# A squared-ReLU perceptron by one level of Strassen's scheme (Winograd's form), and where its sums and the second layer's modulation are made

## What is computed

```python
mod = silu(c) @ w_mod[layer] + b_mod[layer]          # (1024) @ (1024, 6144)
h = rms_norm(x) * (1 + scale1) + shift1
x = x + gate1 * mixer(h)                             # layer 0: gated DeltaNet + attention, layer 1: RWKV-7
h = rms_norm(x) * (1 + scale2) + shift2
x = x + gate2 * (square(relu(h @ w_up[layer])) @ w_down[layer])   # (512,1024)@(1024,4096), (512,4096)@(4096,1024)
```

## Time and profile before

| | us |
|---|---|
| median of 3 runs (range) | 2294.35 (2292.71 to 2296.35) |
| the profiled execution | 2297.16 |
| its span, first to last instruction | 2295.5 |
| mean granted TensorE clock | 0.939 |
| PE busy | 2072.6 (90%) |
| DVE, ACT, POOL busy | 815.3, 395.5, 229.2 |

### The profile page before, as it was taken

How to read it: one execution, slowest core, us unless ns; L and a number is a source line. 1 busy time by engine, 2 the same in 40 slices (tenths; PEclk the granted TensorE clock), 3 DMA queues, 4 the chain that set the end, 5 groups by cost and what they waited for, 6 DMA issues and landing times.

```text
span 2295.5 us, 34406 instructions
## 1 busy us (share of the span) xinstructions
PE 2072.6 (90%) x14797; PEld 1078.1 (47%) x14797; DVE 815.3 (36%) x1449; ACT 395.5 (17%) x601; POOL 229.2 (10%) x145
## 2 busy tenths in 40 slices
PE   1988887876999999999779999999886999999998
PEld 1345455443444444444425666665673344444444
DVE  6656645237435220000163455555542111110000
ACT  1332213455020000000202222223311200000000
POOL 0000000000005787700000000000000000000000
PEclk7889998978999999999789999999996999999999
DMA  6421000010415554422101110110001222222222
GB/s 232 149 83 38 19 32 24 1 37 1 145 62 178 178 169 156 155 73 73 51 10 50 32 32 23 32 32 14 2 3 44 67 71 75 73 73 73 73 73 73
DMA packets 148063, 159.66 MB, mean 70 GB/s; under 512 B 8920, under 2 KB 136411, under 8 KB 147804
## 3 DMA queue, kind: packets, MB, share of 16 engines
q1 hardware_dynamic: 137052, 115.79, 16.2%
q0 software_dynamic: 10880, 41.95, 5.2%
HBM read 155.62 MB, written 2.10 MB: 69 GB/s over the span
## 4 chain that ended last, share of the span: by engine, by line
PE 80%; DVE 11%; ACT 5%; issue 2%; DMA 1%; SPq 0%; DVEq 0%; ACTq 0%
PE PS L449 80%; DVE arena L1356 2%; DVE arena L985 1%; DMA arena<-in_w_mod_dram 1%; DVE arena L1080 1%; ACT arena L1637 1%; ACT arena L1651 0%; DVE arena L1093 0%; ACT L1442 0%; DVE hT L1035 0%; DVE soft L1272 0%; SPq L351 0%; ACT hT L1457 0%; DMA arena<-in_w_in_dram 0%; DVE arena L1159 0%
## 5 line engine op out<-in xcount | busy, mean ns | idle before, releaser
L449 PE MATMUL PS<-arena 64*64 64x64 f32 (+4 forms) x11320 | 1190.9, 291 | 112.9 <-DVE arena L1093 23.4
L449 PEld LDWEIGHTS PS<-arena 64*64 64x64 f32 (+3 forms) x11320 | 665.9, 147 | 665.2 <-issue 537.7
L449 PE MATMUL PS<-hT,arena 128*128 128x512 f32 (+2 forms) x1504 | 683.7, 609 | 31.7 <-ACT hT L1457 12.1
L449 PEld LDWEIGHTS PS<-hT,arena 128*128 128x128 f32 (+2 forms) x1504 | 279.1, 190 | 372.5 <-issue 350.8
L1311 DVE SCALAR_TENSOR_TENSOR xT<-PS,gate_cols,xT 128x512 f32 x24 | 18.0, 751 | 493.6 <-PE PS L449 493.6
L1451 ACT ACTIVATE sq<-xT 128x512 f32<-128x512 f32 x32 | 20.2, 631 | 604.0 <-DVE xT L1311 305.9
L449 PE MATMUL PS<-sq,cst 128*128 128x512 f32 x152 | 84.4, 667 | 36.3 <-ACT sq L1451 30.7
L1746 POOL TENSOR_TENSOR arena<-arena,cond 128x2048 f32<-128x2048 f32 x24 | 86.6, 3609 | 28.4 <-DMA arena<-in_w_mod_dram 27.6
L1320 DVE TENSOR_SCALAR sq<-PS 128x512 f32<-128x512 f32 x32 | 22.1, 692 | 175.1 <-PE PS L449 175.1
L1712 ACT ACTIVATE arena<-PS 128x512 f32<-128x512 f32 x8 | 4.8, 598 | 451.6 <-PE PS L947 449.4
L1336 DVE TENSOR_SCALAR sq<-PS 128x512 f32<-128x512 f32 x32 | 22.1, 692 | 148.5 <-PE PS L449 148.4
(11 more groups left out here) (225 smaller groups left out, 1130.0 us busy)
## 6 DMA issues: line engine op xcount, KB each, us to landing
arena<-in_w_mod_dram POOLq DMA_DIRECT2D x40, 1024.0 KB, 5.8
arena<-in_w_up_dram SPq DMA_DIRECT2D x32, 1024.0 KB, 5.5
arena<-in_w_down_dram SPq DMA_DIRECT2D x32, 1024.0 KB, 5.3
arena<-in_w_mod_dram SPq DMA_DIRECT2D x8, 1024.0 KB, 5.0
arena<-in_w_in_dram SPq DMA_DIRECT2D x16, 512.0 KB, 3.7
arena<-in_w_out_dram SPq DMA_DIRECT2D x4, 1024.0 KB, 7.8
arena<-in_rwkv_w_r_dram SPq DMA_DIRECT2D x8, 512.0 KB, 4.0
arena<-in_rwkv_w_k_dram SPq DMA_DIRECT2D x8, 512.0 KB, 4.4
```

Source lines behind the costliest of these rows:

```text
L449: return pe.matmul(o, l, r, start=first, stop=last)
```

## The change

Each weight matrix is split in two by two quarters (input features, output features), the activations in two by two (input features, tokens 0 to 255 and 256 to 511), and Winograd's seven products take the place of eight. A perceptron is now 32 **units**: 16 for `up`, each making two tiles of 128 features by 512 tokens (`v` and `v + 16`), and 16 for `down`, four in a row (`c` = 0 to 3) adding up two output tiles (`p` and `p + 4`). One unit is seven products of four matmuls of 128 x 128 by **256** columns, each product in a bank of its own (banks 0 to 6). So a perceptron has 32 x 28 = 896 matmuls of 256 columns where it had 512 of 512.

- SyncE (`parts`): four DMAs per unit, 256 KB each with rows of 128 columns, into a ring of two units.
- VectorE: `weight_sums`, four additions of 128 x 512 per unit; `combine`, seven additions of 128 x 256 that each read a bank (in `down` once in four units, with four updates of `xT` more); `token_sums`, once per layer, four operations of 128 x 1024 on `hT` before `up`'s third product.
- ScalarE: copies product 1 out of its bank (`first_product`), and makes ReLU and square of the hidden values, eight operations of 128 x 256 per `up` unit.
- GpSimd: `hidden_sums`: one subtraction of 128 x 256 per `up` unit, and three of 128 x 1024 per `down` unit. It fetches layer 1's modulation weights, whose products VectorE now makes (`late_block`): 16 blocks between the units of layer 0's perceptron, 8 between the tiles of `o1`.
- All nine late blocks of layer 0's own modulation stand between the tiles of `o0`. `mod_sums` is now called with 14, 18 (after `o0`), 32 (before layer 0's last unit) and 16 columns (after `o1`).
- The first weights of `o1` are fetched into a ring of their own once RWKV's last projection is done. `weight_sums` of a perceptron's first unit stands before its norm.

```diff
+UP_UNITS, UNITS = 16, 32
+ORDER = (P1, P2, P4, P6, P7, P5, P3)
+DONE = {p: n + 1 for n, p in enumerate(ORDER)}
+TAKEN = {P2: 1, P6: 2, P7: 3, P4: 4, P5: 6, P3: 7}
+MOD_UNITS = tuple(range(2, 15)) + (18, 20, 22)
...
+            def parts(layer):
...
+                    if v >= 2:
+                        sp.wait_ge(prod_out, 7 * (u - 2) + DONE[P4])
+                        sp.wait_ge(sums_ready, 4 * (u - 1))
...
+                        for z in range(2):
+                            sp.dma_start(dst[:, z], src[:, z]).then_inc(part_landed[u % 2], 16)
...
+            def unit(u):
...
+                for p in ORDER:
+                    if first and q:
+                        if p == P1:
+                            pe.wait_ge(p1_taken, q)
+                        else:
+                            pe.wait_ge(prod_taken, 7 * (q - 1) + TAKEN[p])
+                    if p in (P4, P6, P7):
+                        pe.wait_ge(t_ready, 3 * t_set(u) + {P6: 1, P4: 2, P7: 3}[p])
+                    if p in (P6, P7, P5, P3):
+                        pe.wait_ge(sums_ready, 4 * u + {P5: 1, P6: 2, P7: 3, P3: 4}[p])
+                    a, x = operands[p]
+                    for k in range(4):
+                        if v == 0 and p in (P1, P2):
+                            pe.wait_ge(h_ready, (3 if layer else 1) * KT + 2 * k + 1 + (p == P2))
+                        m = mm(PS[:, p, 0:256], a[:, k], x[:, k], first and k == 0, last and k == 3)
+                    m.then_inc(prod_out, 1)
...
+            for u in range(UNITS):
+                if u == UNITS - 1:
+                    mod_sums(macc1, 32, 3, 7)
+                unit(u)
...
+            def weight_sums(u):
+                dve.wait_ge(part_landed[u % 2], 64 * (u // 2 + 1))
+                if u >= 2:
+                    dve.wait_ge(prod_out, 7 * (u - 1))
...
+                do.tell(tt(o[:, 0], w[:, 1, 0], w[:, 1, 1], ALU.add), sums_ready, 4 * u + 1)
+                do.tell(tt(o[:, 1], o[:, 0], w[:, 0, 0], ALU.subtract), sums_ready, 4 * u + 2)
+                do.tell(tt(o[:, 2], w[:, 0, 0], w[:, 1, 0], ALU.subtract), sums_ready, 4 * u + 3)
+                do.tell(tt(o[:, 3], w[:, 0, 1], o[:, 1], ALU.subtract), sums_ready, 4 * u + 4)
...
+            def token_sums(u):
...
+                dve.wait_ge(h_ready, (4 if layer else 2) * KT)
+                do(tt(b12, b12, b11, ALU.subtract))
+                do.tell(tt(t2, b22, b12, ALU.subtract), t_ready, n + 1)
+                do.tell(tt(t4, b21, t2, ALU.subtract), t_ready, n + 2)
+                do.tell(tt(t3, t2, b11, ALU.subtract), t_ready, n + 3)
...
+            def mlp(layer, hooks):
...
+                    if v == 0:
+                        token_sums(u)
+                    if v == UP_UNITS:
+                        do(dve.tensor_copy(gate_cols[:], modT[:, GATE[1]:GATE[1] + KT]))
+                    if v + 1 < UNITS:
+                        weight_sums(u + 1)
+                    if v < UP_UNITS or (v - UP_UNITS) % 4 == 3:
+                        combine(u)
+                    if v in hooks:
+                        hooks[v]()
...
+            def hidden_sums(layer):
+                for v in range(UNITS):
+                    u = layer * UNITS + v
+                    if 1 <= v <= UP_UNITS:
+                        g = v - 1
+                        pool.wait_ge(hid_ready, 64 * layer + 4 * (g + 1))
+                        do(subtract(hid[:, g, 256:512], hid[:, g, 256:512], hid[:, g, 0:256], ALU.subtract))
+                    if v >= UP_UNITS:
...
+                        if v == UP_UNITS + 1:
+                            pool.wait_ge(prod_out, 7 * (u - 1))
+                        else:
+                            pool.wait_ge(prod_out, 7 * (u - 1 if v == UP_UNITS else u - 2) + DONE[P7])
+                        do.tell(subtract(t2, b22, b12, ALU.subtract), t_ready, n + 1)
+                        do.tell(subtract(t4, b21, t2, ALU.subtract), t_ready, n + 2)
+                        do.tell(subtract(t3, t2, b11, ALU.subtract), t_ready, n + 3)
+                    if layer == 0 and v in MOD_UNITS and MOD_UNITS.index(v) + 2 < 16:
+                        late_fetch(MOD_UNITS.index(v) + 2)
...
-            do.loop(6, 16, lambda i: modulation(view(1), i, 4, 0, mwring1, macc1, 0, 256))
```

More of the change, by code:

```diff
@@ L808, in _ @@
                 pass
[L810 to L814, removed]
+            mod_sums(macc2, 2 * EARLY_BLOCKS, 1, 5)
             def scores(h):
@@ L865, in _, with tile @@
             pe.wait_ge(o_ready, 4)
-            def tile(j, src, first, last, base, slot, mt, ready):
+            def tile(j, src, first, last, base, slot, mt, ready, wring):
                 for k in range(KT):
@@ L934, in _ @@
             pairs(RWKV_PAIRS, GDN_PAIRS, True, rwkv_sums, [xr, xk, xv], lambda: None, lambda m: iter(()))
-            stream("o1", hT, 4, 1)
+            stream("o1", hT, 4, 1, wrings[1])
+            mod_sums(macc1, 16, 4, 5)
             norm_sums(3)
[L937 to L940, removed]
+            for u in range(UNITS, 2 * UNITS):
+                unit(u)
+            pe.wait_ge(x_done, 2 * KT)
             for t in range(TT):
@@ L1304, in _ @@
             take_values(3)
[L1306 to L1314, removed]
@@ L1341, in _, with out_projection @@
-            mod_finish(0, 3, *REST_PARTS[2], at=5)
-            residual("down0", KT, GATE[1])
-            mod_finish(1, 4, 0, 48)
+            def out_projection(name, block, blocks):
+                do(dve.tensor_copy(gate_cols[:], modT[:, GATE[0]:GATE[0] + KT]))
+                at = 0
+                for j in range(KT):
+                    dve.wait_ge(tile_out, TIL[name] + j + 1)
+                    do.tell(stt(xT[:, j], PS[:, j % 4, :], gate_cols[:, j:j + 1], xT[:, j], ALU.mult, ALU.add),
+                            tile_taken, TIL[name] + j + 5)
+                    while at < len(blocks) and at * 7 < len(blocks) * (j + 1):
+                        block(*blocks[at])
+                        at += 1
@@ new lines, in combine, with add, to_x @@
+            def combine(u):
+                layer, v = divmod(u, UNITS)
+                up, q = v < UP_UNITS, pair_of(u)
+                done, n = 7 * u, 7 * q
+                written = 64 * layer + 4 * v
+                p = q % 20 - UP_UNITS
+                def add(o, a, bank, step):
+                    do.tell(tt(o, a, PS[:, bank, 0:256], ALU.add), prod_taken, n + step)
+                def to_x(tile_, t, value, last):
+                    x = xT[:, tile_, t * 256:(t + 1) * 256]
+                    ins = stt(x, value, gate_cols[:, tile_:tile_ + 1], x, ALU.mult, ALU.add)
+                    if last:
+                        do.tell(ins, x_done, layer * KT + DOWN_TILES.index(tile_) + 1)
+                    else:
+                        do(ins)
+                dve.wait_ge(p1_taken, q + 1)
+                dve.wait_ge(prod_out, done + DONE[P2])
+                if up and v:
+                    dve.wait_ge(hid_ready, written)
+                add(c11, p1s, P2, 1)
+                if not up:
+                    to_x(p, 0, c11, False)
+                dve.wait_ge(prod_out, done + DONE[P6])
+                add(mid, p1s, P6, 2)
+                dve.wait_ge(prod_out, done + DONE[P7])
+                add(u3, mid, P7, 3)
+                add(c21, u3, P4, 4)
+                if not up:
+                    to_x(p + 4, 0, c21, False)
+                dve.wait_ge(prod_out, done + DONE[P5])
+                add(mid, mid, P5, 5)
+                add(c22, u3, P5, 6)
+                if not up:
+                    to_x(p + 4, 1, c22, True)
+                dve.wait_ge(prod_out, done + DONE[P3])
+                add(mid, mid, P3, 7)
+                if not up:
+                    to_x(p, 1, mid, True)
@@ new lines, in mlp @@
+            def mlp(layer, hooks):
+                base = layer * UNITS
+                for v in range(UNITS):
+                    u = base + v
+                    if v == 0:
[8 more added lines that the diff above has]
+                        hooks[v]()
@@ L1423, in _ @@
                   lambda m: iter(()))
-            residual("o1", KT, GATE[0])
+            out_projection("o1", late_block, [(b, 5 if b == 23 else None) for b in range(16, 24)])
+            mod_finish(1, 4, 32, 48, at=5)
+            weight_sums(UNITS)
             norm(3)
-            relu2("up1")
-            residual("down1", KT, GATE[1])
+            mlp(1, {})
         @block.scalar
```

235 lines of the change are left out of this document (148 added, 87 removed).

## The result

The changed kernel takes 2189.91 us (median of 4 runs, 2189.16 to 2192.43), the kernel before, on the same chip, 2295.35 (2292.71 to 2296.41): a ratio of 0.9544, interval 0.9528 to 0.9561. That is 105.4 us less; forecast were 113.3 less and 2181, in a range of 2165 to 2232.

The account below looks back on a forecast made before the run. TensorE, busy 90% of the span, was taken as the bound. Savings of 60.1 us in layer 0, 51.6 in layer 1's perceptron and 1.6 around `o1`, together 113.3 off 2294.35, gave 2181 us, range 2165 to 2232.

Parts of the forecast that it names:

- A record of 256 columns: Perceptron matmuls: half a 512-column record's time, weight load hidden, 0.216 us each, so 12.1 us a unit.
- Nobody holds TensorE up in a unit: Perceptron units: work of VectorE, ScalarE, GpSimd and SyncE is hidden beside TensorE's 12.1 us.
- The start of `up`: Unit 0: product 3 waits for VectorE's token sums, 9.3 us after the first block; unit 0 takes 19 us.
- The seam to `down`: First `down` unit: TensorE waits 3.8 to 5 us for GpSimd, then loses to the clock; 6 us per layer.
- Modulation sums: Before layer 0's last unit: 32 columns, 64 one-column records, partly at the lower clock, take 9.6 us.
- the half clock in the last unit: Layer 0's unit 31 starts at the lower clock behind the one-column sums, costing 2 us.
- the norm: Behind layer 0's perceptron: takes 7.6 us, as after `o0`, not 9.54.
- The step that failed: In `o0`: nine modulation blocks on VectorE are hidden between tiles; late fetches cost 0 to 6 us, taken as 0.
- A second step: After `o0`: 18 modulation columns are 8 more than before and cost 1.9 us before the norm.
- Small waits in every unit: Rival in the perceptrons: semaphores or the port cost 1 us a unit, 64 us, giving 2245; chance 13%.
- The clock between products: Rival in the perceptrons: waits between banks lower TensorE's clock, 2.7 us a unit, 173 us, giving 2354; chance 3%.
- GpSimd as the bound: Rival in `down`: port conflicts stretch GpSimd's three sums to 18.4 us a unit, 202 us, giving 2383; chance 2%.

Follow-up runs that it names:

- the new order: Changed kernel, but GpSimd makes its three sums for unit 16 before the subtraction for the last hidden tile: 2176.45 us against 2189.9.
- both rings: Two versions of the changed kernel with other fetches of layer 0's modulation blocks during `o0`, the deep ring and the paced ring: 2190.50 and 2184.84 us.
- the paced ring: Changed kernel, layer 0's late modulation blocks each fetched in `o0` when the block three before is used, at most three under way: 2184.84 us against 2189.9.
- the deep ring: Changed kernel, modulation blocks 9 to 13 of layer 0 given own buffers, all fetched after `o0`'s first tile: 2190.50 us against 2189.9.

## Why the prediction was right

The mechanism was right, and most terms within a microsecond. **A record of 256 columns** was taken at 0.216 from two rows of attention's scores, and is 0.216. **Nobody holds TensorE up in a unit**: doubling a product cost its records and nothing more (55.1 for 55.4 us). **The start of `up`** was 9.3 us to product 3, measured 9.27; unit 0 as a whole 18.0, not 19. **The seam to `down`** was 3.8 to 5 with 2 for the clock, measured 4.2 and 5.0 with 2.5 and 2.4; the reason given, GpSimd standing behind the subtraction for the last tile, is shown by the new order. **Modulation sums** 9.6 and 9.56, **the half clock in the last unit** 2 and 2.6, **the norm** 7.6 and 7.7, **`o1`** 5.4 sooner and 5.5. So perceptron 0 was forecast at 419.3 us with its sums and norm and took 420.2, perceptron 1 400.1 and took 400.3.

Part of that closeness is luck. Unit 0 was 1 us shorter than taken and the seam 0.7 and 1.4 longer than its 6. The modulation sums were read from a wrong split: in the kernel before the clock was at its upper level for the first 4 of 17.28 us (some 35 records) and not for half the 96 records, and in the changed one it fell after 4.5 us. The same 64 records took 9.3 to 11.0 us in the other kernels here that make them in one go.

**The step that failed** is the one on `o0`: "Nine blocks of 4.0 between eight tiles, 36 + 6 of 57 us, are hidden ... If the fetches there land late, cost 0 to 6 us; I take 0." VectorE waited for five of the blocks, up to 4.3 us and 10 in all, since a ring of two lets a fetch go only when a block is used; it landed in up to 9.8 us, against a median of 5.8 on the page before, while the projection's weights and the first units' 2 MB were fetched too. The longest of these waits, and the end of the last block:

```profile
619.07 0.35 DVE L1119 TENSOR_SCALAR arena<-arena,cond 128x256 f32<-128x256 f32 x1 [4.27 <-DMA arena<-in_w_mod_dram]
...
639.80 0.17 DVE L1129 COPY cond_t<-cond 128x8 f32<-128x8 f32 x1
```

The last block ended 3.1 us after the projection, and after that pause the one-column sums took 7.1 us instead of 4.3. These two, 3.1 + 2.8, went when the fetches came in time (both rings: 4.18 for the sums, no wait before them). The term's own upper end, 6, left out the clock behind the wait.

A second step failed beside it: "The 18 columns after `o0` are 8 more: 1.9 us before the norm". The norm sums took 9.6, and 9.2 to 9.4 in the two rings, without any wait: the eight columns more cost not only their 1.9 us but 1.5 to 1.7 of lower clock behind them. In sum the stage grew by 9.7 where 1.9 was forecast, 7.8 too much; the paced ring took 6.3 of that back.

The norm sums after `o1` took 9.2 us instead of 7.8, 1.4 that the prediction had not, behind 32 one-column records; the clock was 1.00 in those and 0.50 from 1765 to 1767 us. The first 32 records of `o1` took 16.6 us instead of 15.6, though TensorE's wait before them was shorter; why is not shown.

The median missed by 8.9 us, of which 1.0 is the kernel before, 1 us slower in this comparison than in the table ahead of the prediction. In the profile the saving was 106.8 instead of 113.3: 7.8 too little in `o0`, 1.2 from perceptron 0 to perceptron 1 and 1.1 in the perceptrons, and 3.7 more than forecast before `o0` and at the end, where no saving was counted.

**The rivals.** Small waits in every unit: none, 880 records without a wait. The clock between products: granted 1.00 in the stretch below; seven banks in turn without waits keep it at 1.00 as four did. The rule of the Trainium skill, TensorE: Matmul & The Clock Gate, section on the second failure mode (PSUM-queue cycling), by which such cycling can keep the clock switching, did not decide here. Columns of the window of the changed kernel: start:end, its length, then busy us (and instructions) of PE, PEld, DVE, ACT and POOL, the granted clock, and the share and GB/s of DMA:

```profile
1786.00:1976.00 190.00, 189.90 (x880) 167.22 (x881) 98.30 (x176) 57.77 (x140) 14.18 (x15) 1.00 0.31 89
```

GpSimd as the bound: its three sums took 2.35 to 2.68 each, under 8.1 of 12.1 us. In the conflict VectorE was the one that waited; GpSimd lost 0.3 per operation, not 3.8.

## What to carry to other kernels

Where TensorE bounds a stage and its records of half the width cost half, a level of Strassen's scheme gives nearly the full eighth (perceptron 1: 451.7 to 400.3 us), if every sum has another engine and a unit of slack; look then at the seams, where that slack isn't there yet. A queue that works in order must have the urgent work first: one subtraction ahead of three sums cost 6.8 and 7.4 us in the two layers. For work moved into a stage, count how late its data can land among everything else that is fetched there, and what the clock costs after the wait; ask for data as it is used, not all at once; and don't lengthen a run of tiny matmuls without looking at the clock behind it.

## What the runs showed of the hardware that was not expected

- Sixteen one-column records between dense units leave TensorE's clock at its upper level, and so did 20 before the norm sums; 36 in a row, with no wait before them, were followed by norm sums 1.5 to 1.7 us longer at the lower clock; 64 in a row cost 1.9 us in themselves and 2.6 in the unit behind them.
- VectorE's and GpSimd's additions, side by side, take turns, one operation each: 0.69 us became 2.72, 2.35 became 2.67. VectorE's short addition waits for nearly a whole one of GpSimd's; GpSimd's loses less than one of VectorE's.
- Runs whose code is the same up to `o0` came to it at 579.2 to 585.4 us. The traces show that most of the difference is there long before attention: the first records of layer 0's mixer that read `sq` start at 140.4 us with the paced ring, 142.0 in the changed kernel and 145.7 with the deep ring, and `o0` follows 438.6 to 439.7 later. Twelve matmul records that start at 103 to 105 us took 6.4, 8.7 and 9.2 us in these three, part of it; why is not shown. Stages, not spans, are to be compared between single profiles of this kernel.
